# Seven block products for twelve units of a fused two-block layer: u, zs and the second gates

## The reference, cut to what matters

```python
h = rmsnorm_2(x, norm_g[l])
proj = h @ w_in[l]
q, k, v, za, u, vs, zs, gm = jnp.split(proj, IN_SPLITS_2, axis=-1)
a = window_sink_attention(q, k, v, att_sinks[l])      # q and k after partial rope
a = (a * jax.nn.silu(za)) @ w_att_out[l]
sgo = chunked_spatial_gating(gelu(u), gelu(vs), sg_w[l], sg_b[l], sg_ln_g[l], sg_ln_b[l])
sgo = (sgo * jax.nn.silu(zs)) @ w_sg_out[l]
ga, gs = jnp.split(jax.nn.sigmoid(gm + b_merge[l]), N_BRANCHES, axis=-1)
x = x + (ga * a + gs * sgo) @ w_o[l]
return rmsnorm_2(x, final_g)
```

## Time and profile before

| what | value |
|---|---|
| time, median of 3 runs | 1308.45 us (1308.4 to 1308.55) |
| span of the profiled execution | 1307.0 us |
| instructions | 18557 |
| TensorE busy | 1300.3 us, 99% |
| TensorE weight loads | 1099.5 us, 84% |
| VectorE busy | 695.3 us, 53% |
| ScalarE busy | 569.8 us, 44% |
| GpSimd busy | 657.8 us, 50% |

### The profile page before, as it was taken

One profiled execution on the slowest core, in us unless ns is written; L12 is line 12 of the kernel. 1 busy time (PEld: TensorE's weight loads), 2 busy tenths in 40 slices (PEclk: granted clock), 3 DMA queues, 4 the chain that ended last, 5 costly groups with the idle time before them and its releaser, 6 DMA issues.

```text
span 1307.0 us, 18557 instructions
## 1 busy us (share of the span) xinstructions
PE 1300.3 (99%) x7208; PEld 1099.5 (84%) x7208; DVE 695.3 (53%) x1121; ACT 569.8 (44%) x881; POOL 657.8 (50%) x488
## 2 busy tenths in 40 slices
PE   9999999999999999999999999999999999999998
PEld 8877877887888899889989988877778888888887
DVE  4674544555454598348736867666544322342234
ACT  6223534566533555225523546345555224342233
POOL 4463333434553588658866865443334453335441
PEclk9999999999999999999999999999999999999999
DMA  6333151413222333334333333332211222313221
GB/s 205 97 114 105 41 153 51 144 41 121 81 73 97 97 98 98 107 88 114 112 98 97 90 137 113 110 98 73 98 65 65 97 97 78 116 65 108 95 87 65
DMA packets 143614, 126.93 MB, mean 97 GB/s; under 512 B 4464, under 2 KB 138736, under 8 KB 143536
## 3 DMA queue, kind: packets, MB, share of 16 engines
q1 hardware_dynamic: 143184, 125.66, 30.9%
q10 hardware_dynamic: 352, 0.19, 0.1%
HBM read 120.46 MB, written 2.10 MB: 94 GB/s over the span
## 4 chain that ended last, share of the span: by engine, by line
PE 99%; DMA 1%; ACT 0%; DVE 0%; issue 0%; SPq 0%; ACTq 0%
PE gemm L748 21%; PE gemm L749 21%; PE gemm L756 20%; PE gemm L1060 5%; PE gemm L1056 5%; PE gemm L1055 5%; PE gemm L806 2%; PE gemm L805 2%; PE gemm L809 2%; PE gemm L772 2%; PE gemm L773 2%; PE gemm L778 2%; PE mix L1182 1%; PE mix L1170 1%; PE mix L1159 1%; DMA xtm<-x 1%
## 5 line engine op out<-in xcount | busy, mean ns | idle before, releaser
L623 POOL TENSOR_TENSOR wlo<-raw,whi 128x512 fp32r<-128x512 f32 x344 | 463.0, 1377 | 412.5 <-ACT whi L1340 400.2
L748 PE MATMUL gemm<-hh,whi 128*128 128x512 f32 x808 | 319.4, 395 | 0.0
L749 PE MATMUL gemm<-hl,whi 128*128 128x512 f32 x808 | 315.0, 390 | 0.0
L756 PE MATMUL gemm<-hh,wlo 128*128 128x512 f32 x808 | 201.2, 390 | 0.0
L1340 ACT ACTIVATE whi<-raw 128x2048 fp32r<-128x2048 f32 x83 | 158.4, 1909 | 71.8 <-PE gemm L756 52.2
L748 PEld LDWEIGHTS gemm<-hh,whi 128*128 128x128 f32 x808 | 151.7, 188 | 35.5 <-issue 4.2
L749 PEld LDWEIGHTS gemm<-hl,whi 128*128 128x128 f32 x808 | 151.8, 188 | 30.7 <-issue 0.2
L756 PEld LDWEIGHTS gemm<-hh,wlo 128*128 128x128 f32 x808 | 151.2, 188 | 31.2
L619 POOL TENSOR_TENSOR wlo_b<-raw_b,whi_b 128x512 fp32r<-128x512 f32 x16 | 20.6, 1288 | 145.2 <-ACT whi L1340 145.2
L651 POOL TENSOR_TENSOR wlo<-raw,whi 128x512 fp32r<-128x512 f32 x60 | 83.6, 1418 | 6.7 <-ACT whi L1549 6.6
L1055 PE MATMUL gemm<-t_hi,whi 128*128 128x256 f32 x320 | 80.2, 283 | 0.0
(11 more groups left out here) (502 smaller groups left out, 2574.6 us busy)
## 6 DMA issues: line engine op xcount, KB each, us to landing
raw<-w_in SPq DMA_DIRECT2D x53, 1024.0 KB, 5.1
raw<-w_gu SPq DMA_DIRECT2D x44, 512.0 KB, 5.0
raw<-w_o SPq DMA_DIRECT2D x8, 1024.0 KB, 5.0
raw<-w_down SPq DMA_DIRECT2D x16, 512.0 KB, 4.5
raw_b<-w_branch SPq DMA_DIRECT2D x16, 256.0 KB, 5.5
raw<-w_ao SPq DMA_DIRECT2D x4, 1024.0 KB, 4.9
raw<-w_so SPq DMA_DIRECT2D x4, 1024.0 KB, 4.9
raw<-w_in SPq DMA_DIRECT2D x7, 512.0 KB, 4.5
```

Source lines behind the costliest of these rows:

```text
L623: last = nc.gpsimd.tensor_tensor(a(wlo), a(raw), as_f32(a(whi)), ALU.subtract)
L748: mm(bank[:, :], w, xh[:, k, :], start=(k == 0), stop=False)
L749: mm(bank[:, :], w, xl[:, k, :], start=False, stop=False)
L756: last = mm(bank[:, :], wlo_[:, s, k, col:col + P], xh[:, k, :], start=False, stop=(k == kts - 1))
```

## The change

- The eight units of stage n_uz (four u, four zs) and the four gate units of stage n_gs become seven-product units, in groups of ten (n_uz to n_gs + 1) and two (n_gs + 4, n_gs + 5). Stage n_gs now runs two gate units, two projection units, and the same again.
- Their input is x normalized fully, `hn_a` and `hn_b`: eight multiplications of `xT` by a gain and by `r2` on VectorE in the third pair of stage n_ga (`normed_input`), then three sums of its parts (`input_sums`; a fourth overwrites a part). ScalarE makes the high parts of the sums before it splits the weights of the stage's last unit, and those of the four quadrants after its sigmoids; VectorE makes the remainders in the fourth pair (`input_rests`, `split_rests`), with the weight sums of the first unit between, all ahead of the pair's two gate products. The scalings by R of these 24 tiles go.
- The four layer-norm tiles move to the first two pairs of stage n_ga, two in each.
- GpSimd multiplies u by zs after the activations (`gated_product`); VectorE multiplies the mixed tile by that (`mixed_out`).
- S4 of these units lies in SBUF (`s4_u`), S1 and S2 in M[2] and M[3]. Many tiles have other places in SBUF, and the scratch for dynamic DMA is cut to 1024.

```diff
-            gates(n_ga, g2t, False)
+            def normed_input():
+                for k in range(KD):
+                    dst = hn_a if k < 4 else hn_b
+                    last = stt(out=dst[:, k % 4, :], in0=xT[:, k, :], scalar=pcol("ng2", k), in1=r2[:, :], op0=ALU.mult, op1=ALU.mult)
+                last.then_inc(sem("t_made"), 1)
+            def input_sums():
+                a_l, a_r, b_l, b_r = hn_a[:, :, 0:HALF], hn_a[:, :, HALF:], hn_b[:, :, 0:HALF], hn_b[:, :, HALF:]
+                dve.wait_ge(sem("t_made"), 5)
+                link(tt(u_sum[:, 0], a_r, a_l, ALU.subtract))
+                tt(u_sum[:, 1], b_r, u_sum[:, 0], ALU.subtract)
+                link(tt(u_sum[:, 2], b_r, a_r, ALU.subtract))
+                tt(a_r, b_l, u_sum[:, 1], ALU.subtract).then_inc(sem("t_made"), 1)
...
             for p in range(4):
-                n = n_uz + 2 * p
+                n = n_ga + 2 * p
                 for j in range(2):
-                    scaled(tiles_before(n) + j, ub[:, j, :])
+                    scaled(tiles_before(n) + j, g2t[:, j, :])
+                if p == 0:
+                    layer_norm_stats()
+                    layer_norm(0)
+                    layer_norm(1)
+                elif p == 1:
+                    layer_norm(2)
+                    layer_norm(3)
+                elif p == 2:
+                    dve.wait_ge(sem("vb_ready"), TT)
+                    normed_input()
+                else:
+                    input_rests()
+                    weight_sums(SECOND[0][0])
+                    split_rests()
+                    sum_rest(SECOND[0][0], S1)
                 for j in range(2):
-                    scaled(tiles_before(n + 1) + j, zb[:, j, :])
+                    m, T = 2 * p + j, tiles_before(n + 1) + j
+                    dve.wait_ge(sem("gm_act"), m + 1)
+                    tile_ready(T)
+                    tt(y2[:, m, :], G[T % 4][:, :], g2t[:, j, :], ALU.mult).then_inc(sem("tile_free"), 1)
+                    dve.wait_ge(sem("tile_free"), T + 1)
+                if p == 2:
+                    input_sums()
```

VectorE's new step after a zs unit, and GpSimd's product:

```diff
+                for j in range(2):
+                    m = 2 * p + j
+                    d = sgt[:, j, :]
                     dve.wait_ge(sem("mixed"), m + 1)
-                    dve.wait_ge(sem("u_act"), m + 1)
-                    link(tt(d, d, ub[:, j, :], ALU.mult))
-                    dve.wait_ge(sem("zs_act"), m + 1)
-                    tt(d, d, zb[:, j, :], ALU.mult).then_inc(sem("sg"), 1)
+                    dve.wait_ge(sem("product"), HIDDEN[-1][-1].w + 1 + m + 1)
+                    tt(d, d, ub[:, j, :], ALU.mult).then_inc(sem("sg"), 1)
+                for j in range(2):
+                    m = 2 * p + j
                     dve.wait_ge(sem("sg_hi"), m + 1)
-                    tt(sgl[:, m, :], d, as_f32(sgh[:, m, :]), ALU.subtract).then_inc(sem("sg_lo"), 1)
+                    tt(sgl[:, m, :], sgt[:, j, :], as_f32(sgh[:, m, :]), ALU.subtract).then_inc(sem("sg_lo"), 1)
```

```diff
+                pool.wait_ge(sem("u_act"), 2 * p + 2)
+                for j in range(2):
+                    pool.wait_ge(sem("zs_act"), 2 * p + j + 1)
+                    nc.gpsimd.tensor_tensor(ub[:, j, :], ub[:, j, :], zb[:, j, :], mult).then_inc(sem("product"), 1)
```

ScalarE in stage n_ga, and TensorE's stages:

```diff
+                    if p == 3 and u == 0:
+                        act.wait_ge(sem("t_made"), 6)
+                        for i in range(3):
+                            fn(u_hi[:, i], u_sum[:, i], ACT.Copy).then_inc(sem("t_hi"), 1)
+                    if p > 0 and 2 * p + u + 1 < 8:
+                        split(n_ga + 2 * p + u + 1)
...
+            first_his(SECOND[0][0])
+            split_input()
+            fourth_hi(SECOND[0][0])
+            sum_hi(SECOND[0][0], S1)
```

```diff
-            unit_fm(n_gs)
-            unit_last_k(n_gs + 1, sgh, sgl, KD, ("sg_lo", 0))
-            pairs_after_first(n_gs, sgh, sgl)
+            for u in SECOND[0]:
+                seven_products(u, normed_2, made if u.first else {})
+                if second_of(u)[0] == "u":
+                    mixing(second_of(u)[1])
+            after_seven(SECOND[0][-1])
+            pe.wait_ge(sem("sg_lo"), KD)
+            for j in range(2):
+                unit_fm(n_gs + 2 + j, sgh, sgl)
+            for u in SECOND[1]:
+                seven_products(u, normed_2, {})
+            after_seven(SECOND[1][-1])
+            for j in range(2):
+                unit_fm(n_gs + 6 + j, sgh, sgl)
```

More of the change, by code:

```diff
@@ L90 @@
     last: bool
+    c0: int
 def build_program(nc, x, par, cst1, cst2a, w_in, w_branch, w_o, w_gu, w_down, w_in2, sg_w, sg_b, ln_g,
@@ L358, in build_program, with sums_of @@
         SEVEN = []
+        def sums_of(kind):
+            return 3 if kind == "hidden" else 2
         def group(kind, n0, count, kt=4):
-            g = [Seven(n0 + i, len(SEVEN) + i, tiles_before(n0 + i), tiles_before(n0), n0 % 2, kt, kind, i, i == 0, i == count - 1)
-                 for i in range(count)]
+            c0 = SEVEN[-1].c0 + sums_of(SEVEN[-1].kind) if SEVEN else 0
+            g = [Seven(n0 + i, len(SEVEN) + i, tiles_before(n0 + i), tiles_before(n0), n0 % 2, kt, kind, i, i == 0, i == count - 1,
+                       c0 + i * sums_of(kind)) for i in range(count)]
             SEVEN.extend(g)
@@ L367, in build_program, with second_of @@
         HIDDEN = [group("hidden", n0 + (0 if f else 2), part - (0 if f else 2)) for f, (n0, part, h0) in enumerate(ffn_units)]
+        SECOND = [group("second", n_uz, 10), group("second", n_gs + 4, 2)]
+        def second_of(u):
+            at = u.n - n_uz
+            if at < 8:
+                return "uz"[at % 2], at // 2
+            return "g", at - 8 if at < 12 else at - 10
         def hidden_of(u):
@@ L595, in _ @@
             stream_pairs(n_uz, (w_in2, I2_U), (w_in2, I2_ZS))
-            stream_pairs(n_gs, (w_in2, I2_GS), (w_so, 0))
+            for half in range(2):
+                for i, (w, c0) in enumerate(((w_in2, I2_GS), (w_so, 0))):
+                    for j in range(2):
+                        n = n_gs + 4 * half + 2 * i + j
+                        slot_free(n)
+                        load(n, cols(w, c0 + (2 * half + j) * UC, UC))
             stream(n_o2, 4, both(tiles_of(w_o2, 0)))
@@ L1223, in _, with normed_2, mixing @@
             pairs_after_first(n_ga, ath, atl)
-            for p in range(4):
-                unit_fm(n_uz + 2 * p)
+            def normed_2(xi, k):
+                if xi < 3:
+                    kt, tok = ((k, slice(0, HALF)), (k + 4, slice(0, HALF)), (k + 4, slice(HALF, SEQ)))[xi]
+                    return hh[:, kt, tok], hl[:, kt, tok]
+                if xi == 6:
+                    return hh[:, k, HALF:], hl[:, k, HALF:]
+                return u_hi[:, xi - 3, k, :], u_lo[:, xi - 3, k, :]
+            made = {A11: ("t_lo", 8), A12: ("t_lo", 9), S1: ("t_lo", 5), A22: ("t_lo", 10), S2: ("t_lo", 6), S3: ("t_lo", 7),
+                    S4: ("t_lo", 11)}
+            def mixing(p):
                 if p == 0:
@@ L2309, in seven_last @@
                 dve.wait_ge(sem("tile_done"), u.T + 2)
-                tt(pair(3 + at, 6 + at), halves_of(bank(u, W)[:, :]), pair(U3, U4), ALU.add).then_inc(sem("tile_free"), 1)
+                if u.kind == "hidden":
+                    tt(pair(3 + at, 6 + at), halves_of(bank(u, W)[:, :]), pair(U3, U4), ALU.add).then_inc(sem("tile_free"), 1)
+                else:
+                    o = out_of(u)
+                    tt(pair2(o + 1, o + 2), halves_of(bank(u, W)[:, :]), pair2(V4, V3), ALU.add).then_inc(sem("tile_free"), 1)
             for f, (n0, part, h0) in enumerate(ffn_units):
```

284 lines of the change are left out of this document (171 added, 113 removed).

## The result

The changed kernel takes 1312.34 us (median of 8 runs, 1312.04 to 1314.23), the kernel before 1308.54 beside it: ratio 1.003, 95% interval 1.0021 to 1.0039. It is slower by 3.8 us; the forecast was 1311.2. The profiled execution's span is 1310.5, 3.5 over before's 1307.0.

The account below looks back on a forecast made before the run. TensorE, busy 1300.3 of 1307.0 us, was taken as the bound. -9.6 + 0.3 + 1.1 + 6.5 + 2.1 + 2.0 + 0.4 = +2.8: span 1309.8, time 1311.2 us; range 1302 to 1314.

Parts of the forecast that it names:

- The long wait: Entry to the group: TensorE waits 6.5 us before the second product of the first u unit, until VectorE's gate product.
- twelve units: Four u, four zs and four second-gate units go from 10.88 to 10.08 us each: 9.6 us less.
- last unit's weights late: Stage n_ga's last unit: ScalarE splits its weights only after copying three sums, so TensorE waits 0.3 us.
- first product: First seven-product unit: waits 1.1 us for the first input remainder and GpSimd's remainders.
- second product: First seven-product unit: waits 6.5 us for the gate product at 1080; bounds 0 and 7.6.
- clock: After the entry gap the clock falls to 1.2 GHz, 4.2 us run at half pace: 2.1 us more; bounds 0 and 3.
- three steps after a zs unit: Steps with mixing: the next unit's banks are freed late, 0 to 0.3 us of wait each, 0.4 in all.
- second gate unit: After the last zs, without mixing, banks come at 13.1 where 11.5 is needed: 2.0 us of wait; bounds 0 and 3.5.
- the turns of VectorE and GpSimd: VectorE operations with both inputs in SBUF alternate with GpSimd's by whole instructions, 2.14 to 2.3 us a turn.
- The rivals without the long wait: No long wait at the entry: 1302 us, chance 0.20. Partial turns, wait near 3 and no clock fall: 1305.5, chance 0.13.
- without turns the wait is 0: Lower bound for the second product's entry wait: without turns the gate product ends before 1072.4.
- its rival: VectorE late at every zs step: silu 1 us later gives three more waits of 1 us, 1314 us; chance 0.12.

Follow-up runs that it names:

- last kernel: Changed kernel with bank-freeing gate product earlier, gated tiles' remainders later, ScalarE's weight split before its sum copies, fourth quadrant's remainder after the fifth product's weight remainder: 1299.23 us.
- gap filled: Changed kernel plus 48 extra matmuls of 256 columns, read by nothing, between first and second product of the first seven-product unit: 1311.86 us.
- small GpSimd work: Changed kernel with eight of GpSimd's nine entry operations done on 8 of 128 columns, so outputs are not the reference's: 1304.47 us.
- split first alone: Changed kernel with one edit: ScalarE rounds the last gate unit's weights before copying the three input sums: 1306.58 us.
- gate products early: Changed kernel with VectorE's first gate product right after the weight sums, the second and the weight remainder after the second input remainder: 1307.18 us.

## Why the prediction was right

The long wait, its cause and the fall of the clock came as forecast, each at its place. That the sum came so near is partly luck: four terms were 1.3 us too high together, two were 1.8 us too low. The terms, forecast against measured:

| term | forecast | measured | from |
|---|---|---|---|
| twelve units | -9.6 | -9.6 | span of the last kernel |
| last unit's weights late | 0.3 | 0 | no such wait |
| first product | 1.1 | 1.0 | waits after |
| second product | 6.5 | 6.0 | waits after |
| clock | 2.1 | 1.7 | 17 matmuls; gap filled: 1.7 |
| three steps after a zs unit | 0.4 | 1.8 | mixing starts: 3 x 0.6 |
| second gate unit | 2.0 | 2.4 | starts 1179.12 and 1187.25: 8.13 for four products of 1.44 |
| sum | +2.8 | +3.3 | span +3.5 |

- **Right:** the pace of the units, the turns of VectorE and GpSimd, the gate product as what is late (forecast 1080; the first of the two in the row at 1078.53 ends near 1079.2), the fall and return of the clock, and that the two sums that free the banks stand behind VectorE's turns inside the group. The rivals without the long wait can be made by an edit each: small GpSimd work gave 1304.47 (1302 named), split first alone 1306.58 (1305.5 named). The first lies 2.5 over its rival mostly by the steps after a zs unit (1.8 against 0.4) and by the bound "without turns the wait is 0": the first product then started at 1070.14, not at 1070.9 or later, so the second waited 1.1 us for a gate product at 1072.09.
- **Mis-sized:** the step "with mixing: 13.2 and 14.7, so 0 to 0.3 of wait, three times". The changed kernel's timeline has the S1 remainder at 1113.73, the sum that frees the second bank at 1114.33 and the last at 1115.97. Counted from the start of the u unit, 1089.62 + 1.73 + 10.08 = 1101.4, they end at 13.0, 13.6 and 15.3, in place of 12.4, 13.1 and 14.9. Half a microsecond on a margin of 0.1 made 0.3 of wait at the second product and 0.2 at the third. The same half microsecond turns the 2.0 of the second gate unit into 2.4. About 0.3 of it is a reading: the forecast counts from TensorE's start of a unit, but its 1.7 is 600.10 + 0.38 - 598.73, from the start of VectorE's last sum. TensorE had started that unit at 598.46 (timeline of TensorE, kernel before), and in the changed kernel, too, VectorE's last sum (1101.75) comes 0.3 after the unit's start, so the two bias sums end at 6.0 in place of 5.7. The rest is in the two products, which last 3.03 us where the forecast has 2.7. The forecast named the margin, and gave its rival a chance, but at a full microsecond.
- **Not there:** the 0.3 for the late split: ScalarE started it at 1057.34, 0.5 sooner than forecast, since the input sums behind the gate products took 1.22 us each and ended at 1054.4.
- **Costed at nothing:** this held for the layer norm, the loads and the second gate group: no profile lists a wait of TensorE there.
- **A sign that did not show:** the page has no clock digit below 9, since 5 us at half clock in a slice of 33 leave over 0.9.
- **Beside the terms:** 0.2 us between their sum and the span. TensorE's waits for the first loads were 0.5 us in this execution and 0.3 in before's; they differ by tenths between executions.

That the clock's fall costs 1.7 us at the entry rests on the trace and on four of the eight runs with the gap filled. Whether it falls after a wait of about 2 us is open: it did in the profiled executions with 2.1 us (split first alone) and 1.9 (GpSimd small; gap filled), and not with 1.9 in those of the changed kernel and of the gate products early. No experiment here varied this wait alone.

## What to carry to other kernels

A change that saves TensorE work can move the limit to whoever prepares its inputs: here 9.6 us saved were given back as 12.9 us of waits for VectorE and of slow clock, all of it removable by order alone. On the engine that is late, put what frees a bank first and what is read last behind it; and look also at the engine beside it, since one statement moved on ScalarE took GpSimd's 8 us run out of VectorE's busiest stretch into an idle one, for 5.8 us. Ask of each wait written into a queue what ready work it holds: here the wait of three copies held a split, from about 1048.9, where it ran with the order changed, to 1057.3.

## What the runs showed of the hardware

- Waits of 1.9 to 2.1 us were followed by the lower clock in some executions and not in others; after the 2.1 us wait it fell as TensorE had already restarted (0.55 in 1074 to 1076, restart at 1073.59), after the 5.95 us wait in the gap itself.
- Executions of one kernel lie in two groups by their mean clock. Medians of the spans: with the gap filled 1308.75 (clock 0.999) and 1310.4 us (0.998), with the gate products early 1305.0 and 1306.4, with GpSimd's work small 1302.5 and 1303.8. The differences are 1.3 to 1.7 us, and the traces have about the same for one fall: 1.7 at the changed kernel's entry; 1.5 at the entry with the split first alone (two products behind the wait take 4.46 us, with GpSimd's work small 2.97); behind the wait in the second gate unit 1.4 with the gap filled (three products take 6.03 us, in the changed kernel 4.63) and 1.3 with GpSimd's work small (two take 4.45, in the changed kernel 3.19). That each of the longer executions had one such fall is likely, but only the profiled ones have a trace.
- What a turn costs VectorE goes with the length of GpSimd's instruction. With GpSimd's entry work small, the three remainders from 1060.26 took 4.52 us beside one full GpSimd operation (1.30 us at 1060.01) and two of 8 columns, 1.0 more than the 3.50 of the split first; an input remainder beside one of 8 columns took 1.28 us, 0.06 to 0.07 more than those alone. The Trainium skill (SBUF — State Buffer, Summary) says that the second to issue blocks until the first finishes; this agrees.
